# Relative-position bias rows built in partition order: 128 stored copies of each line in place of a reversal on TensorE

## The reference, cut to what matters

```python
def _rel_bias(table, q0, n_keys):
    t = q0 + jnp.arange(Q_BLOCK)
    s = jnp.arange(n_keys)
    b = table[_t5_bucket(s[None, :] - t[:, None])]
    return jnp.transpose(b, (2, 0, 1)).astype(jnp.float32)
```

## Time and profile before

| | |
|---|---|
| median of 3 runs | 1207.34 us (1206.68 to 1208.55) |
| the profiled execution | 1206.32 us, its span 1204.5 us |
| busy share of the span | PE 88%, PE weight loads 49%, DVE 29%, ACT 20%, POOL 1% |
| DMA | 446.00 MB, 370 GB/s on average over the span |
| granted TensorE clock, mean | 0.938 |
| attention part of layer 0 | about 0 to 170 us |

### The profile page before, as it was taken

The page is one execution under the profiler, slowest core; times in us unless marked ns, Lnnn a source line. Parts: engine busy times, 40 slices in busy tenths (PEclk is TensorE's granted clock), DMA queues, the critical chain, the costliest instruction groups (busy, mean ns, idle before and its releaser), DMA issues.

```text
span 1204.5 us, 18674 instructions
## 1 busy us (share of the span) xinstructions
PE 1054.3 (88%) x7889; PEld 594.6 (49%) x7892; DVE 344.7 (29%) x966; ACT 235.3 (20%) x578; POOL 18.0 (1%) x49
## 2 busy tenths in 40 slices
PE   9999999987887888778999999999887968787886
PEld 5777564443434343434468765554443434334433
DVE  3445563211111111111247365622111111111112
ACT  1234311111111111111112441121111111111112
POOL 1000100000000000000010000000000000000000
PEclk9999999998888889888999999999988988898899
DMA  8677579999999999999998056899999999999995
GB/s 303 218 278 280 227 271 429 426 427 426 426 428 424 429 425 427 426 427 427 414 389 309 26 221 254 318 426 428 426 426 426 428 425 427 425 425 427 425 429 214
DMA packets 59142, 446.00 MB, mean 370 GB/s; under 512 B 10888, under 2 KB 15536, under 8 KB 32176
## 3 DMA queue, kind: packets, MB, share of 16 engines
q1 hardware_dynamic: 57216, 443.57, 89.6%
q10 hardware_dynamic: 1840, 1.19, 0.3%
HBM read 442.63 MB, written 2.11 MB: 369 GB/s over the span
## 4 chain that ended last, share of the span: by engine, by line
PE 49%; DMA 44%; SPq 3%; DVE 2%; issue 1%; ACT 1%; POOL 0%; POOLq 0%; ACTq 0%; DVEq 0%
DMA ring<-in_w_up 39%; PE pv L1738 11%; PE pj L1396 8%; PE tr L1757 4%; PE pj L1637 4%; DMA arena<-in_w_up 4%; PE lg L1765 4%; PE pj L1765 3%; SPq L577 3%; PE pj L1402 2%; PE pj L1487 2%; PE tr L1725 1%; PE lg L1426 1%; PE pv L1749 1%; PE pj L1608 1%
## 5 line engine op out<-in xcount | busy, mean ns | idle before, releaser
L1738 PE MATMUL pv<-ring,xT 128*32 128x256 f32 x3136 | 287.7, 446 | 84.5 <-DMA ring<-in_w_up 52.2
L1738 PEld LDWEIGHTS pv<-ring,xT 128*32 128x32 f32 x3136 | 141.9, 123 | 188.2 <-issue 140.7
L1235 DVE TENSOR_SCALAR arena<-arena 128x128 f32<-128x128 f32 x64 | 14.5, 227 | 663.5 <-ACT arena L817 663.2
L1765 PE MATMUL lg<-arena 128*128 128x512 f32 x256 | 131.9, 597 | 0.0
L1765 PE MATMUL pj<-arena 128*128 128x512 f32 x256 | 130.7, 592 | 0.0
L656 ACT ACTIVATE arena<-pv 128x256 f32<-128x256 f32 x64 | 24.5, 383 | 512.2 <-PE pv L1738 512.2
L656 ACT ACTIVATE arena<-tr 128x512 f32<-128x512 f32 (+3 forms) x168 | 92.3, 558 | 125.1 <-PE tr L1757 107.0
L1738 PE MATMUL pv<-arena,xT 128*32 128x256 f32 x640 | 88.5, 434 | 19.6 <-DMA ring<-in_w_up 19.6
L1396 PE MATMUL pj<-xT,ring 128*128 128x256 f32 x448 | 100.6, 381 | 0.0
L1396 PEld LDWEIGHTS pj<-xT,ring 128*128 128x128 f32 x448 | 83.9, 190 | 12.9 <-issue 1.0
L1757 PE MATMUL tr<-ring,arena 128*32 128x512 f32 x696 | 84.2, 594 | 1.9 <-issue 1.9
(11 more groups left out here) (226 smaller groups left out, 933.2 us busy)
## 6 DMA issues: line engine op xcount, KB each, us to landing
ring<-in_w_up SPq DMA_DIRECT2D x48, 2048.0 KB, 38.8
ring<-in_w_gate SPq DMA_DIRECT2D x46, 2048.0 KB, 43.6
ring<-in_w_down SPq DMA_DIRECT2D x42, 2048.0 KB, 42.2
arena<-in_w_down SPq DMA_DIRECT2D x14, 2048.0 KB, 42.3
arena<-in_w_gate SPq DMA_DIRECT2D x12, 2048.0 KB, 46.0
ring<-in_w_in SPq DMA_DIRECT2D x10, 2048.0 KB, 20.0
arena<-in_w_up SPq DMA_DIRECT2D x8, 2048.0 KB, 38.1
ring<-in_w_out SPq DMA_DIRECT2D x4, 2048.0 KB, 16.2
```

What stands on the lines that cost most here:

```text
L1738: ins = mm(gu_ps[i * CAP:(i + 1) * CAP, :], xg[:, j, c:c + CAP], w, start=(j == 0), stop=(j == KD - 1), tile_position=(0, i * CAP), skip_g ...
L1765: ins = mm(acc[t][half], pgT[:, b, t, :], y[:, 512 * half:512 * half + 512], start=False, stop=last, skip_group_check=True)
```

## The change

The HBM tensor for the lines becomes 128 times as large. The store writes each of the 8 lines 128 times, one copy after the other (8 x 128 x 1536 bytes, 1.57 MB), reading the line's one partition over and over by a step of 0. The load starts at element 127 and steps by 383, one less than a line, from partition to partition, so partition p begins at 127 - p of copy p. The reversed unit matrix, its load, the four groups of products on PE, the four copies on ACT and the semaphores between them go. SP waits for `lines_out` before the `w_out` loads, and POOL for `bias_in` before its mask.

```diff
-          w_gate, w_up, w_down, norm_final, consts_d, onehot_d, flip_d, out_d):
-    lines_d = nc.dram_tensor("bias_lines", (8, LINE), F32, kind="Internal")
+          w_gate, w_up, w_down, norm_final, consts_d, onehot_d, out_d):
+    lines_d = nc.dram_tensor("bias_lines", (8, P * LINE), F32, kind="Internal")
...
-        flip = ring[:, 7, 1024:1024 + P]
...
                 if l < 1:
-                    sp.wait_ge(flip_read, 4)
+                    sp.wait_ge(lines_out, 16)
...
                 if l < 1:
-                    pool.wait_ge(flip_read, 4)
+                    pool.wait_ge(bias_in, 16)
                     nc.gpsimd.memset(bias[0:64, 0:8, SEQ - CHUNK:], NEG).then_inc(bias_ready, 1)
...
-            act.dma_start(flip, flip_d).then_inc(flip_in, 16)
...
                 act.wait_ge(line_copied, 1)
-                act.dma_start(lines_d.ap(), lines).then_inc(lines_out, 16)
+                act.dma_start(bass.AP(lines_d, 0, [[P * LINE, 8], [LINE, P], [1, LINE]]), spread(lines, 1, P)).then_inc(lines_out, 16)
...
                 act.wait_ge(lines_out, 16)
-                act.dma_start(bias[:, 0:8, :], bass.AP(lines_d, 0, [[1, P], [LINE, 8], [1, SEQ]])).then_inc(bias_in, 16)
+                act.dma_start(bias[:, 0:8, :], bass.AP(lines_d, P - 1, [[LINE - 1, P], [P * LINE, 8], [1, SEQ]])).then_inc(bias_in, 16)
...
-                def flipped(g):
-
-                    if l == 0:
-                        act.wait_ge(flip_done, g + 1)
-                        copy(bias[:, 2 * g:2 * g + 2, :].rearrange("p h k -> p (h k)"), lg[:, g % 2]).then_inc(flip_read, 1)
...
                 dots_out(4); dots_out(5)
-                flipped(0); flipped(1)
                 dots_out(6); dots_out(7)
                 pair(10, 2)
-                flipped(2); flipped(3)
...
-                def flips(g):
-
-                    if l == 0:
-                        if g >= 2:
-                            pe.wait_ge(flip_read, g - 1)
-                        for i in range(2):
-                            ins = mm(lg[:, g % 2, SEQ * i:SEQ * i + SEQ], flip, bias[:, 2 * g + i, :], start=True, stop=True)
-                        ins.then_inc(flip_done, 1)
...
                 if l == 0:
                     pe.wait_ge(line_copied, 1)
-                    pe.wait_ge(flip_in, 16)
-                    pe.wait_ge(bias_in, 16)
-                flips(0)
-                flips(1)
...
                 pair(2, BK - BQ)
-                flips(2)
-                flips(3)
                 pe.wait_ge(qk_ready, l + 1)
```

More of the change, by code:

```diff
@@ L377, in trunk @@
         half_in, more_consts_in = sem("half_in"), sem("more_consts_in")
-        consts_in, tables_in, flip_in, lines_out, bias_in = (
-            sem("consts_in"), sem("tables_in"), sem("flip_in"), sem("lines_out"), sem("bias_in"))
+        consts_in, tables_in, lines_out, bias_in = sem("consts_in"), sem("tables_in"), sem("lines_out"), sem("bias_in")
         x_in = [sem(f"x_in{t}") for t in range(TOK)]
@@ L383, in trunk @@
         line_done, line_copied, bias_ready = sem("line_done"), sem("line_copied"), sem("bias_ready")
-        flip_done, flip_read = sem("flip_done"), sem("flip_read")
         gain_in, small_in, final_in = sem("gain_in"), sem("small_in"), sem("final_in")
@@ L1936 @@
     arrays["const_buckets"] = bucket_one_hot()
-    arrays["const_flip"] = np.ascontiguousarray(np.eye(P, dtype=np.float32)[::-1])
     args = [nc.dram_tensor(n, a.shape, mybir.dt.from_np(a.dtype), kind="ExternalInput").ap()
```

## The result

The changed kernel takes 1222.88 us (median of 4 runs, 1222.48 to 1223.18), the kernel before 1207.01 us beside it: 15.9 us more, a ratio of 1.0137 with a 95% interval of 1.0123 to 1.0150. The profiled execution took 1222.89 us, its span is 1221.1.

The account below looks back on a forecast made before the run. PE was taken to bound the stretch up to 160 us. A 13.5 us stall plus 2.6 for the clock minus 4.86 removed gave +11.2, so 1218.5 us against the 1207.34 median; range 1202 to 1228, the forecast's own 1212 to 1230.

Parts of the forecast that it names:

- The work that goes: Ahead of the first logits: reversal products of 1.96 and 1.73 us and a 1.17 us PE wait leave the path, 4.86 us.
- Both readings: In attention: PE's 1.17 us wait is for the bias load, and DVE keeps 1.9 and 1.1 us of slack.
- Number of engines: In the bias store: 8 DMA engines with 128 pieces each, from the old store's 8 completion packets.
- When the store lands: In the bias store: start at 26.5 us plus 29.5 us, half of the upper bound, so it lands at 56.0.
- upper bound: For the bias store: eight partitions give 26.8 GB/s together, so 1.573 MB take 58.7 us.
- Taking turns: On the store's engines: a store piece alternates with a `w_in` piece, 147 ns a pair, 18.9 us for 128 pairs.
- The clock: On PE after its stall: the clock at 0.50 for 6 us, 1.2 instead of 2.4 GHz, costs 2.6 us more.
- One for one: From attention to the kernel's end: a shift of attention moves the end by the same amount.
- The `w_in` stream: In the weight loads beside the store: pushed back by up to 8.1 us, third chunk has 9.1 us room, costed at nothing.
- Rival 2: In the bias store: engines limit, not partitions; lands at 45.4 us, 2.9 us stall, total 1206.1 us; chance 0.18.
- Rival 1: In the bias store: it lands before 42.5 us and is hidden, total 1202.5 us; chance 0.15.

## Why the prediction was right, and where it was off

It said 1218.5 us, slower, and 1222.9 was measured. The mechanism is the one it named: ACT stands still for the store, PE idles ahead of L1548 (now L1527) and its clock falls. Three terms were off in size, and they can be set side by side from PE's rows.

- **The work that goes**, -4.86 us: measured 4.71, in three kernels alike (27.56 us against 32.27). Both readings behind it held. The 1.17 us were a wait for the bias load: the wait for ACT's copy is still in these kernels and costs nothing. And DVE was not late: with the wait on SP it still waits 1.10 us for the first logits, as the prediction had it.
- **Number of engines**, 8, read off the completion packets: held, 1032 packets.
- **When the store lands**, 56.0 us: it was 60.8. This term was mis-sized, and it carries nearly all of the miss. Its start came too early: the prediction took 26.5 us from a window of 26 to 28, but narrower windows show the old store's packets between 27.0 and 28.0, and the new one's from 28.0 on. And 29.5 us for the bytes, half of an upper bound (which would be 29.35), was too short: the packets took 32 us, from 28.0 to 60.0, and another 0.8 us went by up to the landing. That the half came so near is partly luck. No row then showed two shared ways; the store alone does, by its 51 GB/s, which give 30.8 us. PE's stall became 18.37 us instead of 13.5.
- **Taking turns**: 126 packets of the store and 122 of the weights between 52 and 56 us are a store piece for about every weight piece, a pair every 254 ns on each of the 8 engines (8 x 4 us / 126), and 128 of them make 32.5 us. The prediction's 147 ns for a pair came from engines that nothing held up.
- **The clock**, 2.6 us: measured 1.51 + 4.45 us of chain against 0.65 + 3.46, 1.85 us. This term was too large by 0.75 us, and it hid as much of the longer stall.
- Sum by measured terms: 18.37 + 1.85 - 4.71 = +15.5 us at the first logits, and 15.9 at the end. One for one held.
- **The `w_in` stream**, costed at nothing: right in the outcome, wrong in the size. I allowed 8.1 us of push-back. The load issued at 21.1 us landed 19.6 us later than the load of that place in the kernel before (20.5 us after its issue there, 40.0 in the changed kernel), the next one 18.7. The weights on the store's engines were held back with it: from 52 to 56 us the 8 engines together moved 109 GB/s, store and weights, where 8 engines of the full stream move half of 389. The third chunk, which had 9.1 us of room, was not hit (29.6 us), and the later ones had the room.
- **Rival 2** (engines, not partitions, are the limit) came true in the kernels with lines two and four apart, where the store landed 22.6 and 22.7 us after its issue, at 46.6 us with lines two apart, where 45.4 was said. Its price was wrong, since I took about 3 us of idleness as too short for the clock; the stalls of 4.3 us took 6.6 and 7.3 us with the clock, and by their single runs the kernels are slower than the one before, not level with it.
- **Rival 1** (the store is hidden) is what the kernel with lines on all partitions does, at 1201.6 us where 1202.5 was said.

That the wait on ACT and not the traffic cost 21.4 us is shown, by the kernel that moves only this wait and its load. That the shared way and not the pieces made the store slow is shown too, by those with the partition step as the only difference. The store took 4.1 us longer in the changed kernel than alone, 36.7 against 32.6. The queue's packets split this: 2.6 us are the start, the first packet passing 4.0 us after the issue instead of 1.4, and most of the rest is the moving, 32 us against 30.8. So taking turns packet by packet explains only the smaller part. That the start is late because the weight stream fills the engines is argued; the slow store without that stream was not tried in its own place.

## What to carry to other kernels

Ask of every transfer that grows who stands behind its wait, and put a wait for a slow transfer into the program of an engine that has nothing else to do: this moved the time by 21 us with no byte changed. A DMA that reads few partitions can be limited by them, not by its bytes: the same 1.57 MB took 32.6 us from eight neighbours and 10.2 from eight partitions four apart. Make the data on all 128 partitions if TensorE can do so cheaply (the same product with repeated columns, 0.91 us instead of 0.81), and look at the outermost count: 8 gave 8 engines here, 128 gave 16. When work in a stage is left out to price it, read the price at a point ahead of the first decision that depends on data.

## What the runs showed that I had not expected

- PE's clock was at 0.50 after an idle stretch of 4.3 us with lines two apart, and the products behind it took 2.3 us more; with lines four apart the same 4.3 us cost 3.0 more, and in the changed kernel 18.4 us of idleness cost 1.7 more (all by PE in time; 1.85 by the chain). The length of the idle stretch did not set this price. In all three the clock had fallen while PE idled, and what counted was how long it stayed low after the work came back: by the windows 4.7 us (47.7 to 52.4), 5.9 us (49.9 to 55.9) and 3.4 us (61.9 to 65.4). The price is half of that each time, as it is when work runs at 1.2 instead of 2.4 GHz.
- Half of the DMA engines, held up by the store's few partitions, slowed the other queue's traffic on them to less than a third (0.24 MB in 4 us, 60 GB/s, where 8 engines of the full stream move 195), and the load that spans all engines ended with its slowest: 40 us from issue to landing instead of 20.5.
- Three expert loads more, and 27 us, from bias rows in another order: the kernel's time depends on its data, since an expert with more than 32 tokens costs one more pass.
